# Expert passes of a two-layer decoder trunk filled with blocks of 32 rows: 45 passes in place of 52

## The reference

```python
scores = jax.nn.sigmoid((xt @ router_w).astype(jnp.float32))
...
_, eidx = lax.top_k(jnp.where(emask, biased, -jnp.inf), TOP_K)     # 8 of 64
...
def swiglu(x, w1, w3, w2):
    return (jax.nn.silu(x @ w1) * (x @ w3)) @ w2
def expert_block(acc, blk):
    tok, wt, e = blk
    y = swiglu(x_pad[tok], w1[e], w3[e], w2[e])
    return acc.at[tok].add(y * wt[:, None].astype(y.dtype)), None
```

## Time and profile before

| | |
|---|---|
| timed executions | 2985.59, 2987.11, 2992.85 us |
| span of the profiled execution, first to last instruction | 2981.4 us |
| median of the timed runs less that span | 5.7 us |
| TensorE (PE) busy | 2661.9 us, 89% of the span |
| mean granted TensorE clock | 0.944 |
| VectorE, ScalarE, GpSimd busy | 1037.0, 628.8, 360.3 us |
| DMA | 658.03 MB, mean 221 GB/s |

### The profile page before, as it was taken

How to read it: one execution, slowest core, us unless ns; L and a number is a source line. 1 busy time by engine, 2 the same in 40 slices (tenths; PEclk the granted TensorE clock), 3 DMA queues, 4 the chain that set the end, 5 groups by cost and what they waited for, 6 DMA issues and landing times. The chain is left out here.

```text
span 2981.4 us, 31993 instructions
## 1 busy us (share of the span) xinstructions
PE 2661.9 (89%) x11495; PEld 1506.3 (51%) x11496; DVE 1037.0 (35%) x2058; ACT 628.8 (21%) x1263; POOL 360.3 (12%) x396
## 2 busy tenths in 40 slices
PE   6998989899859999999974999999868999999974
PEld 3565556556734444444432476676744444444431
DVE  1434334423361222221138444444352222221138
ACT  0112030311221211221111333433221112111211
POOL 0000001000001111111100122121101111111101
PEclk9999989999969999999986999999978999999987
DMA  6532416243157999999955121221257999999954
GB/s 260 163 109 87 136 49 182 69 127 96 36 224 273 364 382 387 384 378 389 373 228 170 39 83 44 71 70 36 73 197 276 357 386 393 381 385 381 372 236 181
DMA packets 180803, 658.03 MB, mean 221 GB/s; under 512 B 30408, under 2 KB 92200, under 8 KB 125376
## 3 DMA queue, kind: packets, MB, share of 16 engines
q1 hardware_dynamic: 129872, 525.43, 45.9%
q0 software_dynamic: 37632, 104.92, 10.1%
q10 hardware_dynamic: 13168, 25.89, 3.0%
HBM read 624.64 MB, written 60.85 MB: 230 GB/s over the span
## 5 line engine op out<-in xcount | busy, mean ns | idle before, releaser
L1662 PE MATMUL moe_py<-weights_w,moe_hT 128*128 128x512 f32 (+1 forms) x1040 | 375.9, 595 | 3.5 <-ACT moe_hT L1239 3.5
L1648 PE MATMUL moe_ph<-weights_w,moe_xT 128*128 128x512 f32 x832 | 373.4, 602 | 1.8 <-DVE moe_xT L1449 1.8
L1648 PE MATMUL moe_pr<-weights_w,moe_xT 128*64 128x512 f32 (+1 forms) x1248 | 369.7, 596 | 1.1 <-DVE moe_xT L1449 1.1
L862 PE MATMUL attn_proj<-core_hT,attn_w_w 128*128 128x512 f32 x768 | 341.4, 606 | 15.4 <-issue 12.9
L1449 DVE COPY moe_xT<-moe_tx 128x512 f32<-128x512 f32 x104 | 71.9, 691 | 752.1 <-PE moe_tx L1621 752.1
L862 PEld LDWEIGHTS attn_proj<-core_hT,attn_w_w 128*128 128x128 f32 x768 | 149.1, 195 | 201.1 <-issue 197.1
L1648 PEld LDWEIGHTS moe_ph<-weights_w,moe_xT 128*128 128x128 f32 x832 | 155.6, 192 | 179.8 <-issue 179.8
L1648 PEld LDWEIGHTS moe_pr<-weights_w,moe_xT 128*64 128x64 f32 (+1 forms) x1248 | 134.3, 154 | 194.7 <-issue 193.8
L2226 PE MATMUL gdn_pj<-core_hT,gdn_w_w 128*128 128x512 f32 x512 | 226.4, 596 | 0.0
L1290 POOL DMA_INDIRECT y_rows<-moe_ysb,moe_yidx x104 | 105.5, 1015 | 993.1 <-ACT moe_ysb L1248 850.7
L1662 PEld LDWEIGHTS moe_py<-weights_w,moe_hT 128*128 128x128 f32 (+1 forms) x1040 | 140.2, 169 | 163.6 <-issue 156.4
(11 more groups left out here) (366 smaller groups left out, 3018.4 us busy)
## 6 DMA issues: line engine op xcount, KB each, us to landing
weights_w<-in_expert_w_dram SPq DMA_DIRECT2D x384, 1024.0 KB, 12.0
attn_w_w<-in_attn_w_in_dram SPq DMA_DIRECT2D x36, 1024.0 KB, 8.7
weights_w<-y_rows SPq DMA_DIRECT2D x32, 1024.0 KB, 5.3
attn_ada_w<-in_ada_w_dram POOLq DMA_DIRECT2D x64, 384.0 KB, 5.9
gdn_w_w<-in_gdn_w_in_dram SPq DMA_DIRECT2D x16, 1024.0 KB, 6.0
normNone_w<-in_ada_w_dram SPq DMA_DIRECT2D x8, 1536.0 KB, 6.4
attn_swp<-attn_raw ACTq DMA_DIRECT2D x192, 64.0 KB, 2.1
gdn_ada_w<-in_ada_w_dram POOLq DMA_DIRECT2D x32, 384.0 KB, 3.6
```

The source lines that it names most:

```text
L862: last = nc.tensor.matmul(proj[n % 2][:], w[:, j % SLOTS, kk, half_ * P:(half_ + 1) * P], c.hT[:, kk, :], start=kk == 0, stop=kk == KT - 1)
L1648: last = nc.tensor.matmul(ph[b][at, :], xT[:, b, k, at], w13[:, n % UP, :, k], start=k == 0, stop=k == KT - 1)
L1662: last = nc.tensor.matmul(py[n][at, :], hT2[:, b, k, at], w2[:, load % DOWN, k, half(n)], start=k == 0, stop=k == 1)
```

## The change

An expert now gets rows in blocks of 32 by its rank: ranks 0 to 2 and 4 to 9 four blocks (128), rank 3 eight (256), ranks 10 to 37 three (96), ranks 38 to 63 two (64). The blocks are laid one behind another through the passes, and an expert may begin in one pass and go on in the next. That fills 45 passes of 128 rows to the last row (5760 rows). A piece of an expert in a pass is a `Part`, of 128, 64 or 32 rows, at a place that is a multiple of its size. The ranks come in the order 0, 1, 2, and then groups of four ranks with 96 rows, one with 128, four with 64. The work of a pass, its queues and its slots stay as they are.

```diff
-FULL, DOUBLE, PASSES = 38, 3, 52
+BLK = 32
+DOUBLE, FOURS, THREES = 3, 10, 38
...
+def blocks_of(rank):
+
+    if rank == DOUBLE:
+        return 2 * P // BLK
+    return 4 if rank < FOURS else 3 if rank < THREES else 2
...
 def expert_passes():
 
-    passes, ranks = [], []
-    ahead, behind = iter(range(FULL)), iter(range(FULL, NE))
...
+    order = list(range(DOUBLE))
+    fours, threes, twos = list(range(DOUBLE, FOURS)), list(range(FOURS, THREES)), list(range(THREES, NE))
+    while fours or threes or twos:
+        order += threes[:4] + fours[:1] + twos[:4]
+        fours, threes, twos = fours[1:], threes[4:], twos[4:]
+    passes, at = [[]], 0
+    for load, rank in enumerate(order):
+        first, left = 0, BLK * blocks_of(rank)
+        while left:
+            if at == P:
+                passes.append([])
+                at = 0
+            n = next(n for n in (P, P // 2, BLK) if n <= left and at % n == 0)
+            passes[-1].append(Part(rank, load, first, at, n))
+            first, left, at = first + n, left - n, at + n
...
-        room = np.where(e < FULL, P, P // 2) + P * (e == DOUBLE)
+        room = BLK * np.array([blocks_of(rank) for rank in range(NE)])
...
             def one_hots(p):
-                ps = passes[p]
-                for n, r in enumerate(ps.ranks):
-                    r = NE if ps.start else r
-                    last = one_hot(pos[:, :, r:r + 1], p % 2, n * ps.rows, ps.rows)
+                for part in passes[p]:
+                    r, first = (NE, part.first - P) if part.first >= P else (part.rank, part.first)
+                    last = one_hot(pos[:, :, r:r + 1], p % 2, part.at, first, part.n)
...
                 for k in range(KT):
-                    for i, n in enumerate(ps.loads):
-                        at = slice(i * ps.rows, (i + 1) * ps.rows)
-                        last = nc.tensor.matmul(ph[b][at, :], xT[:, b, k, at], w13[:, n % UP, :, k], start=k == 0, stop=k == KT - 1)
+                    for part in passes[p]:
+                        at = slice(part.at, part.at + part.n)
+                        last = nc.tensor.matmul(ph[b][at, :], xT[:, b, k, at], w13[:, part.load % UP, :, k],
+                                                start=k == 0, stop=k == KT - 1)
...
                 for n in range(2):
                     for k in range(2):
-                        for i, load in enumerate(ps.loads):
-                            at = slice(i * ps.rows, (i + 1) * ps.rows)
-                            last = nc.tensor.matmul(py[n][at, :], hT2[:, b, k, at], w2[:, load % DOWN, k, half(n)],
+                        for part in passes[p]:
+                            at = slice(part.at, part.at + part.n)
+                            last = nc.tensor.matmul(py[n][at, :], hT2[:, b, k, at], w2[:, part.load % DOWN, k, half(n)],
                                                     start=k == 0, stop=k == 1)
```

More of the change, by code:

```diff
@@ L951, in attention_stage, with __init__ @@
     st.close(gathers=True, beside=ring.st)
[L954 to L959, removed]
-def expert_passes():
-    passes, ranks = [], []
-    ahead, behind = iter(range(FULL)), iter(range(FULL, NE))
[L967 to L987, removed]
+def blocks_of(rank):
+    if rank == DOUBLE:
+        return 2 * P // BLK
+    return 4 if rank < FOURS else 3 if rank < THREES else 2
+class Part:
+    def __init__(self, rank, load, first, at, n):
+        self.rank, self.load, self.first, self.at, self.n = rank, load, first, at, n
+def expert_passes():
+    order = list(range(DOUBLE))
[13 more added lines that the diff above has]
+            first, left, at = first + n, left - n, at + n
+    last = {part.load: p for p, parts in enumerate(passes) for part in parts}
+    return passes, order, last
+PASSES = len(expert_passes()[0])
 class ExpertWeights:
@@ L1056, in moe_stage @@
     passes, load_rank, last_pass = expert_passes()
+    loads = [sorted({part.load for part in parts}) for parts in passes]
     UP, DOWN = ew.UP, ew.DOWN
@@ L1210, in _ @@
             for b in range(2):
-                sp.wait_ge(y_out[b], 16 * (PASSES // 2))
+                sp.wait_ge(y_out[b], 16 * ((PASSES + 1 - b) // 2))
             for m in range(TT * TOPK // YG):
@@ L1248, in _ @@
                     nc.scalar.copy(ysb[:, p % 2, half(n)], py[n][:]).then_inc(y_ready, 1)
-            act.wait_ge(y_out[0], 16 * (PASSES // 2))
+            act.wait_ge(y_out[0], 16 * ((PASSES + 1) // 2))
             act.wait_ge(y_out[1], 16 * (PASSES // 2))
@@ L1307, in _ @@
             for b in range(2):
-                pool.wait_ge(xg_in[b], 16 * (PASSES // 2))
-                pool.wait_ge(y_out[b], 16 * (PASSES // 2))
+                pool.wait_ge(xg_in[b], 16 * ((PASSES + 1 - b) // 2))
+                pool.wait_ge(y_out[b], 16 * ((PASSES + 1 - b) // 2))
             def block(j):
@@ L1425, in _, with one_hot @@
             ch.sync()
-            def one_hot(col, b, first, n):
-                return nc.vector.tensor_tensor(onehot[:, b, :, first:first + n],
-                                               iota[:, 0:n].rearrange("p (a n) -> p a n", a=1).broadcast_to([P, TT, n]),
+            def one_hot(col, b, at, first, n):
+                return nc.vector.tensor_tensor(onehot[:, b, :, at:at + n],
+                                               iota[:, first:first + n].rearrange("p (a n) -> p a n", a=1).broadcast_to([P, TT, n]),
                                                col.broadcast_to([P, TT, n]), ALU.is_equal)
             def one_hots(p):
-                ps = passes[p]
-                for n, r in enumerate(ps.ranks):
-                    r = NE if ps.start else r
-                    last = one_hot(pos[:, :, r:r + 1], p % 2, n * ps.rows, ps.rows)
+                for part in passes[p]:
+                    r, first = (NE, part.first - P) if part.first >= P else (part.rank, part.first)
+                    last = one_hot(pos[:, :, r:r + 1], p % 2, part.at, first, part.n)
                 last.then_inc(hot_ready, 1)
@@ L1525, in further_blocks @@
                 ch.do(nc.vector.tensor_scalar(ovi[0:1, 0:OVB], ovf[0:1, 0], float(NE - 1), None, ALU.min))
-                ch.do(nc.vector.tensor_scalar(ovf[:, 2], ovf[:, 0], float(FULL), -float(P // 2), ALU.is_ge, ALU.mult))
+                ch.do(nc.vector.tensor_scalar(ovf[:, 2], ovf[:, 0], float(THREES), -float(BLK), ALU.is_ge, ALU.mult))
+                ch.do(nc.vector.tensor_scalar(ovf[:, 3], ovf[:, 0], float(FOURS), -float(BLK), ALU.is_ge, ALU.mult))
+                ch.sync()
+                ch.do(nc.vector.tensor_tensor(ovf[:, 2], ovf[:, 2], ovf[:, 3], ALU.add))
+                ch.sync()
                 ch.do(nc.vector.tensor_scalar(ovf[:, 3], ovf[:, 0], float(DOUBLE), float(P), ALU.is_equal, ALU.mult))
@@ L1557, in _ @@
             for b in range(2):
-                dve.wait_ge(xg_in[b], 16 * (PASSES // 2))
-                dve.wait_ge(y_out[b], 16 * (PASSES // 2))
+                dve.wait_ge(xg_in[b], 16 * ((PASSES + 1 - b) // 2))
+                dve.wait_ge(y_out[b], 16 * ((PASSES + 1 - b) // 2))
             further_blocks()
@@ L1566, in block @@
                 dve.wait_ge(ov["pcol"], j + 1)
-                one_hot(pcol[:].rearrange("p (t o) -> p t o", o=1), 0, 0, P).then_inc(ov["hot"], 1)
+                one_hot(pcol[:].rearrange("p (t o) -> p t o", o=1), 0, 0, 0, P).then_inc(ov["hot"], 1)
                 dve.wait_ge(ov["idxp"], j + 1)
@@ L1636, in rows_of @@
                     pe.wait_ge(idx_ready, 2 * p)
-                rows(p % 2, [(i * ps.rows, ps.rows, lambda t, r=r: num[:, t, r]) for i, r in enumerate(ps.ranks)], idx_done)
+                rows(p % 2, [(part.at, part.n, lambda t, r=part.rank: num[:, t, r]) for part in passes[p]], idx_done)
             def up_of(p):
-                ps, b = passes[p], p % 2
-                for n in ps.loads:
+                b = p % 2
+                for n in loads[p]:
                     pe.wait_ge(w13_in[n % UP], 32 * (n // UP + 1))
```

## The result

The changed kernel takes 3288.05 us (median of 4 runs, 3286.75 to 3293.19) against 2986.35 us for the kernel before on the same chip: a ratio of 1.1006, 95% interval 1.099 to 1.1022. It is slower by 302 us where I forecast +209 (3196 us, range 2895 to 3265). The direction and the price of a mixed pass came out as forecast; the time lies outside the range. Of the missing 92 us, the rest of the document finds 75 and leaves 17 in part open.

What follows compares the result with a forecast made beforehand. TensorE bounds, DMA close behind. Per layer, 14 three-part passes add 193.9 us, seven dropped passes save 83.2 and small DMA waits some 6: +104.7, over two layers +209, so 3196 us; range 2895 to 3265.

Steps and rivals of the forecast that it cites:

- TensorE sets the pass, DMA close behind: MoE passes: PE busy 495.01 of 500 us, DMA share 0.96; a pass takes 11.88 us.
- a stream at no limit: Rival 1 with weight loads never limiting: -83 us a layer, 2821 us; chance 0.05 for below 2895.
- Shapes take turns, 0.14 us for each change: Three-part passes: 64- and 32-column tiles never overlap, two changes per k; +13.85 us a pass, 14 a layer; chance 0.56.
- The value 0.05 for the longer first instruction: Part of each shape change's 0.14 us, beside a 0.09 us hole; the middle between nothing and 0.12.
- Rival 3: Three-part passes: first instructions of all parts run before the second ones, four changes per k; 3293 us, chance 0.07.
- I expect no wait there.: Weight loads at the closest place: 5 MiB in about 17 us is 310 GB/s, under the 383 sustained before.
- The prediction's own sign of being wrong: Profile after: the forecast is wrong if PE waits for weights or a 32-column tile starts within 0.1 us of a 64-column one.
- The small DMA waits: PE's waits for indices, 4.8 us in 450, go: some 6 us less in a layer.
- Rival 1: Three-part passes: tiles of different width run side by side and the weight stream decides; 2929 us; chance 0.27 in all.
- the bounds of the price of a change of shape: Three-part passes: from no hole, 3105 us, to 0.21 us for a change, 3250 us.

Runs made afterwards that it cites:

- e1: The changed kernel with the 64-row part of a three-part pass given as two tiles of 32, so one shape per pass: 2936.77 us.
- e10: e8 with only half of w2 loaded from the fifth expert on (outputs not the reference's): 2831.45 us.
- e4: The kernel before, with the second expert of each two-expert pass given as two tiles of 32 columns beside the first's 64: 3334.36 us.
- e2: The changed kernel with all k steps of the 32-row parts issued first, then those of the 64-row part: 3211.54 us.
- e3: The changed kernel with each w2 load issued one expert later in SyncE's queue: 3213.47 us.
- e5: The kernel before, with both experts of a two-expert pass given as two tiles of 32 columns each, four of one shape: 2984.08 us.
- e6: e1 plus the edit of e3, the w2 load one expert later: 2926.65 us.
- e8: e1 plus the w2 load one expert later and the two-expert passes laid apart: 2919.62 us.

## Why the prediction was right and wrong

- **TensorE sets the pass, DMA close behind.** Right. With seven passes gone and one shape, the margin of DMA is all that is left: 2937 us in e1, not the 2821 of a stream at no limit (e10, with fewer bytes, gets 2831).
- **Shapes take turns, 0.14 us for each change.** Right in every term: 15.88 for 16.0 us, 7.9 for 8.0, +13.6 for +13.85 with `rows_of`. With these prices e4 was forecast at 3333 and took 3334. The value 0.05 for the longer first instruction was a guess between nothing and 0.12; e2 puts the whole change at 0.13.
- **Rival 3, four changes for a k.** The measured 3288 us is close to its 3293, and that is chance: by this rival an `up_of` would last 8 x 2.28 = 18.2 us and it lasts 15.88, and the close-up shows the four instructions of 32 columns together, two changes for a k. A time alone would have confirmed the wrong mechanism.
- **"I expect no wait there."** This is the step that failed. I worked out the closest place as bytes over time, 5 MiB in 17 us, as if each load were issued when its slot is free. It is issued when everything ahead of it in SyncE's queue is issued, and one of those was the w2 load that waits for a `down_of`. I had the place of that `down_of` wrong by a pass, and I had not carried its own new length, 8 us, into the queue. Measured price: 75 us of the 92 (e3: 3288 to 3213). In layer 0 of the changed kernel 27 us are waits and some 11 us the slower `up_of` behind them; layer 1 has five such waits too. The prediction's own sign of being wrong, PE waiting for weights, is met. The first hint was in the rows I cited: SP's queue waited 501.7 us for moe_py, the end of a `down_of`.
- **The small DMA waits.** I took 6 us a layer off. They went (PE's row for the indices is gone), but the steps without a long part came out at 11.9 to 12.3 us and not 11.74. In e3 the first to the last `up_of` takes 718 us in layer 0 and 719 us in layer 1 for the 711 of the forecast, with some 2 us of waits left in each, and that is most of the 17 us by which e3 stands above 3196. The longest of these steps are those with the `rows_of` of a three-part pass in them, whose 0.25 us the sum had. For the rest I suspect the many more passes that change between 64-column tiles and the full-width transposes, 0.1 us or so each time; no run takes that apart.
- **Rival 1.** Wrong for the changed kernel, but its arithmetic is within 8 us of e1: it is the time of the same plan without a mix of shapes.
- **The range.** It reached to 3265 on the bounds of the price of a change of shape. It had no term for a wait for weights, since I had set that to nothing with one sentence; without the 75 us of that wait, e3's 3213 lies inside it.

## What to carry to other kernels

Count what a packing does to the shapes of the array tiles, not only how many rows it fills: tiles of one shape ran four at a time for the price of one, while a second shape made the same columns take turns, and cutting the wide part to the narrow shape turned +10% into -1.6%. When an instruction becomes longer, follow the in-order queue whose next entry waits for it, and look at every load that stands behind that entry. And a time that agrees with a rival is no evidence for it until its close-up does.

## What the runs showed of the hardware

- Tiles of 128 x 64 and 128 x 32 on disjoint columns do not overlap (changed kernel, e4); each change of shape costs about 0.13 us (e2), 0.09 us of it a hole. Four tiles of 128 x 32 run together at 0.43 us an instruction of 512 float32 columns, and 64 weight loads fit beside an `up_of` of 7.0 us (e5).
- An idle time of 5.35 us on PE was followed by an `up_of` that took 17.49 us in place of 15.95, at a granted clock of 0.90 over the stretch; in the idle time the clock went from 1.00 to 0.50 (changed kernel, pass 16).
- The DMA engines gave 400 to 406 GB/s over 400 us at a share of 0.99 to 1.00 (e1, e6, e8), and 422 over 17 us (changed kernel).
